# Routed experts: rows added to the output by accumulating scatters, in place of a stored table and a combining stage

## The reference

```
hn  = rmsnorm(h, g_ffn)
pg_top, g_idx = top_k(softmax(hn @ w_rg + b_rg), 1)           # 4 groups, the best one
pe_top, e_idx = top_k(softmax(le of that group), 2)           # its 8 experts, the best two
wts = pg_top * pe_top / sum(pe_top)
yb  = (silu(x @ w_gate[e]) * (x @ w_up[e])) @ w_down[e]       # blocks of 128 rows, one expert each
y   = h + sum over the row's two experts of wts * yb
```

## Time and profile before

| | us |
|---|---|
| median of 3 runs | 4226.6 (4226.56 to 4235.43) |
| the profiled execution | 4223.9 |
| its span | 4222.4 |
| expert blocks, from the first Silu to the last copy out of PSUM | 3133.8 to 4105.9 |
| `combine`, from its first load to the end of the span | 4111.9 to 4222.4 |

### The profile page before, as it was taken

One profiled execution on the slowest core, in us unless ns is written; L12 is line 12 of the kernel. 1 busy time (PEld: TensorE's weight loads), 2 busy tenths in 40 slices (PEclk: granted clock), 3 DMA queues, 4 the chain that ended last, 5 costly groups with the idle time before them and its releaser, 6 DMA issues. The chain is left out here.

```text
span 4222.4 us, 58476 instructions
## 1 busy us (share of the span) xinstructions
PE 3404.8 (81%) x20680; PEld 2601.9 (62%) x20729; DVE 2026.5 (48%) x2607; ACT 1367.8 (32%) x2483; POOL 741.7 (18%) x552
## 2 busy tenths in 40 slices
PE   7988759999978888835868996688758999989980
PEld 5777647777756666522426774377647777777760
DVE  3666635555544333331116662233266766675634
ACT  4555433333325323311212322244213433333320
POOL 1333200000000000022100001011114444453423
PEclk9999879999989888966878997788769999999995
DMA  6667543333333111225423332232257967786748
GB/s 223 234 230 236 202 157 138 131 133 138 135 105 96 56 41 51 66 66 168 147 82 112 126 118 91 79 96 97 87 180 248 335 242 254 270 299 217 284 188 319
DMA packets 302568, 683.64 MB, mean 162 GB/s; under 512 B 83355, under 2 KB 95051, under 8 KB 296238
## 3 DMA queue, kind: packets, MB, share of 16 engines
q1 hardware_dynamic: 229910, 448.38, 31.0%
q0 software_dynamic: 53936, 192.71, 13.4%
q10 hardware_dynamic: 18576, 40.51, 2.5%
HBM read 522.60 MB, written 193.16 MB: 170 GB/s over the span
## 5 line engine op out<-in xcount | busy, mean ns | idle before, releaser
L136 PE MATMUL inu_po<-inu_w,inu_nT 128*128 128x512 f32 (+1 forms) x680 | 253.8, 373 | 57.6 <-DVE inu_nT L131 42.1
L2674 POOL TENSOR_TENSOR ex_down<-ex_down_raw,ex_down 128x2048 fp32r<-128x2048 f32 x32 | 205.5, 6422 | 455.7 <-ACT ex_down L2750 455.7
L137 PE MATMUL inu_po<-inu_w,inu_nT 128*128 128x512 f32 (+1 forms) x680 | 247.6, 364 | 0.0
L138 PE MATMUL inu_po<-inu_w,inu_nT 128*128 128x512 f32 (+1 forms) x680 | 247.5, 364 | 0.0
L535 DVE TENSOR_REDUCE att_res<-att_score 128x4 f32<-128x1024 f32 (+1 forms) x96 | 92.5, 988 | 272.3 <-DMA tmp_att<-att_res 221.7
L607 PE MATMUL att_outp<-att_va,att_pT 128*128 128x65 f32 x1200 | 184.5, 300 | 46.9 <-DVE att_pT L542 46.4
L2777 ACT ACTIVATE ex_late<-ex_py 128x512 f32<-128x512 f32 x96 | 52.3, 597 | 485.0 <-PE ex_py L138 485.0
L607 PEld LDWEIGHTS att_outp<-att_va,att_pT 128*128 128x128 f32 x1200 | 170.1, 216 | 63.6 <-DVE att_pT L542 57.8
L136 PE MATMUL inq_po<-inq_w,inq_nT 128*128 128x512 f32 x408 | 192.9, 473 | 19.0 <-DVE inq_w L1082 19.0
L136 PE MATMUL ex_py<-ex_down,ex_hT 128*128 128x512 f32 x384 | 155.9, 406 | 57.0 <-POOL ex_down L2674 44.4
L248 POOL DMA_DIRECT2D inu_big<-tmp_u x256 | 137.5, 538 | 298.9 <-DVE inu_big L324 252.9
(11 more groups left out here) (570 smaller groups left out, 8414.6 us busy)
## 6 DMA issues: line engine op xcount, KB each, us to landing
ex_gate_raw<-in_w_gate SPq DMA_DIRECT2D x32, 2048.0 KB
ex_up_raw<-in_w_up SPq DMA_DIRECT2D x32, 2048.0 KB, 12.0
ex_down_raw<-in_w_down POOLq DMA_DIRECT2D x32, 2048.0 KB, 9.3
inu_big<-tmp_u POOLq DMA_DIRECT2D x256, 192.0 KB, 3.5
tmp_yb<-ex_late ACTq DMA_DIRECT2D x48, 512.0 KB, 7.6
tmp_nT<-inu_nT SPq DMA_DIRECT2D x17, 1024.0 KB, 4.9
inq_nT<-tmp_nT SPq DMA_DIRECT2D x17, 1024.0 KB, 5.0
out_win_k<-in_cache_k SPq DMA_DIRECT2D x8, 2032.0 KB
```

The lines of the kernel that those rows point to most:

```text
L136: pe.matmul(out, ah, bh, start=start, stop=False)
L137: pe.matmul(out, ah, bl, start=False, stop=False)
L138: return pe.matmul(out, al, bh, start=False, stop=stop)
L2674: return eng.tensor_tensor(half["d"][:, 1, k], raw["d"][:, k], half["d"][:, 0, k].bitcast(F32), ALU.subtract)
```

## The change

The stage `combine` and the scratch tensors `yb`, `i_dst`, `wts` and `h2` go. `attend_memory` writes the residual rows straight to the output `y`. The scratch rows `hn` become 1024 + 32 numbers wide: behind each row lie its 32 expert weights, 30 of them zero (`dense`), and a row of zeros stands in front of all rows, for padding. `dense` is made by DVE (three operations of 128x544, and four small ones that stood later before), stored by SP. The gathers bring 4224 bytes a row instead of 4096. ACT copies the block's column of weights to `shares` and uses it as the scale of the copies out of PSUM. In place of the store to `yb`, POOL issues an indirect DMA that adds the block's 128 rows to `y` in memory. Padding rows are added to the rows behind the last real one, for which `y` has one more tile; their lane-wise row numbers are made by five small DVE operations. Since a row's two experts may lie in neighbouring blocks, each add waits for the one before it to have landed. The zero stores go.

```
@@ SP @@
-                sp.wait_ge(E["placed"], 1)
-                sp.dma_start(t["i_dst"], dsti[:]).then_inc(E["saved"], 16)
+                sp.wait_ge(E["zero_ok"], 1)
+                sp.dma_start(t["hn"][0:1, :], zero[0:1, 0:D + NE]).then_inc(E["dense_out"], 16)
+                sp.wait_ge(E["dense_ok"], 1)
+                sp.dma_start(t["hn"][1:, D:].rearrange("(n p) e -> p n e", p=P), dense).then_inc(E["dense_out"], 16)
...
-                def nothing(b):
-                    sp.dma_start(t["yb"][b], zero).then_inc(E["zero_out"], 16)
@@ POOL @@
+                pool.memset(zero, 0.0).then_inc(E["zero_ok"], 1)
+                pool.wait_ge(E["zero_ok"], 1)
+                for u, half_of in enumerate((slice(0, P // 2), slice(P // 2, P))):
+                    pool.dma_start(t["y"][NT, half_of], zero[half_of, 0:D]).then_inc(E[f"y_out{u}"], 16)
+                pool.wait_ge(E["dense_out"], 32)
                 pool.wait_ge(E["idx_ok"], 1)
                 for u in range(SLOTS):
-                    gather(u, idx[:, u:u + 1])
-                pool.memset(zero, 0.0).then_inc(E["zero_ok"], 1)
+                    gather(u, start[:, u:u + 1])
...
+                pool.wait_ge(E["rows_ok"], 1)
+
+                def add(i, u, b):
+                    pool.wait_ge(E["y_ok"], 2 * b + 4)
+                    pool.sem_inc(E["seen"], 1)
+                    pool.wait_ge(E[f"y_out{1 - u % 2}"], i * 32 + (u + 1) // 2 * 16 + 16)
+                    pool.sem_inc(E["seen"], 1)
+                    pool.indirect_dma_start(t["y"].rearrange("n p d -> (n p) d"), bass.IndirectOffsetOnAxis(ap=spot[:, u, 1:2].bitcast(U32), axis=0),
+                                            y[:, u % 2, :], None, compute_op=ALU.add).then_inc(E[f"y_out{u % 2}"], 16)
                 def work(i, u, b):
                     pool.wait_ge(E["x_turned"], b + 1)
-                    pool.tensor_copy(spot[:, u, :], idx[:, bass.ds(b + SLOTS, 1)]).then_inc(E["spot_ok"], 1)
+                    pool.tensor_copy(spot[:, u, :], rows_of[:, bass.ds(b, 1), :].rearrange("p n a -> p (n a)")).then_inc(E["spot_ok"], 1)
+                    pool.wait_ge(E["shares_ok"], b + 1)
...
+                    add(i, u, b)
@@ ACT @@
                     act.wait_ge(E["gate_mm"], b + 1)
+                    act.activation(shares[:, u % 2], xb[:, u, bass.ds(expert(act, b) + D, 1)], ACT.Copy).then_inc(E["shares_ok"], 1)
                     act.wait_ge(E["hh_ok"], b + 1)
                     act.activation(sg, gu[:, 0, :], ACT.Silu).then_inc(E["sg_ok"], 1)
...
                     for n in range(2):
-                        act.activation(y[:, u % 2, 512 * n:512 * n + 512], py[:, n, :], ACT.Copy).then_inc(E["y_ok"], 1)
-                    act.wait_ge(E["y_ok"], 2 * b + 4)
-                    act.dma_start(t["yb"][b], y[:, u % 2, :]).then_inc(E[f"y_out{u % 2}"], 16)
+                        act.activation(y[:, u % 2, 512 * n:512 * n + 512], py[:, n, :], ACT.Copy, scale=shares[:, u % 2]).then_inc(E["y_ok"], 1)
@@ DVE @@
+                for a in range(2):
+                    own.then(V((dense, dense1)[a], oh[:, a], bn(wts[:, a], NE), ALU.mult))
+                V(dense, dense, dense1, ALU.add).then_inc(E["dense_ok"], 1)
                 dve.wait_ge(E["sums_ok"], 1)
...
+                    if a:
+                        dve.wait_ge(E["y_out0"], 16)
+                        dve.wait_ge(E["y_out1"], 16)
+                        dve.wait_ge(E["dense_out"], 32)
...
                 rows(1, 1)
+                own.then(TS(pad[:, 1], pad[:, 0], 0.0, None, ALU.is_equal))
...
+                dve.tensor_copy(rows_of[:, :, 1], pad[:, 0]).then_inc(E["rows_ok"], 1)
                 lower("u", 1)
-def combine(nc, t):
...
```

More of the change, by code:

```diff
@@ L2646, in route_experts @@
         nb, starts, base, cmp = (few[:, k] for k in range(4))
+        dense, dense1 = (byt(spots1[:, D + NE + a * NT * NE:D + NE + (a + 1) * NT * NE]) for a in range(2))
         def read(eng, row, b, top):
@@ L2821, in _ @@
                 own.then(dve.tensor_reduce(m[:, 0], g4[:, 1], AXX, ALU.add))
+                own.then(TS(m[:, 7], m[:, 6], 1.0, None, ALU.add))
+                own.then(V(m[:, 0], m[:, 0], m[:, 7], ALU.mult))
+                own.then(dve.reciprocal(wts[:, 0], m[:, 0]))
+                own.then(V(wts[:, 1], wts[:, 0], m[:, 6], ALU.mult))
+                for a in range(2):
+                    own.then(V((dense, dense1)[a], oh[:, a], bn(wts[:, a], NE), ALU.mult))
+                V(dense, dense, dense1, ALU.add).then_inc(E["dense_ok"], 1)
                 dve.wait_ge(E["sums_ok"], 1)
@@ L2853, in _ @@
                     V(marks[:, a], marks[:, a], bn(tok, NBX), ALU.mult).then_inc(E["marks_ok"], 1)
+                    if a:
+                        dve.wait_ge(E["y_out0"], 16)
+                        dve.wait_ge(E["y_out1"], 16)
+                        dve.wait_ge(E["dense_out"], 32)
                     V(spots[a], row(ib, P), bn(posf[:, 0, a], P), ALU.is_equal).then_inc(E["spots_ok"], 1)
                 dve.wait_ge(E["idx_mm"], 1)
-                dve.tensor_copy(idx[:], th[:, 0:NBX]).then_inc(E["idx_ok"], 1)
-                here = tok[:, 0:1].to_broadcast([P, NE])
+                dve.tensor_copy(start[:], th[:, 0:SLOTS]).then_inc(E["idx_ok"], 1)
+                own.mark(dve.tensor_copy(rows_of[:, :, 0], th[:, SLOTS:SLOTS + NBLK]))
+                own.mark(dve.tensor_copy(pad[:, 0], th[:, 0:NBLK]))
+                own.mark(TS(lane[:, 1:2], tok[:, 0:1], float(SEQ + NS), None, ALU.add))
+                own.then(TS(lane[:, 0:1], tok[:, 0:1], -1.0, None, ALU.add))
+                here = lane[:, 0:1].to_broadcast([P, NE])
                 own.then(V(cmp, ends, here, ALU.is_le))
@@ L2863, in _ @@
                 dve.tensor_reduce(cols[:, 1:2], cmp, AXX, ALU.add).then_inc(E["cols_ok"], 1)
-                own.then(TS(m[:, 7], m[:, 6], 1.0, None, ALU.add))
-                own.then(V(m[:, 0], m[:, 0], m[:, 7], ALU.mult))
-                own.then(dve.reciprocal(wts[:, 0], m[:, 0]))
-                own.then(V(wts[:, 1], wts[:, 0], m[:, 6], ALU.mult))
                 dve.wait_ge(E["plan_mm"], 1)
@@ L2886, in _ @@
                 rows(1, 1)
+                own.then(TS(pad[:, 1], pad[:, 0], 0.0, None, ALU.is_equal))
+                own.then(TS(pad[:, 1], pad[:, 1], lane[:, 1:2], None, ALU.mult))
+                own.mark(TS(pad[:, 0], pad[:, 0], -1.0, None, ALU.add))
+                own.wait()
+                own.then(V(pad[:, 0], pad[:, 0], pad[:, 1], ALU.add))
+                dve.tensor_copy(rows_of[:, :, 1], pad[:, 0]).then_inc(E["rows_ok"], 1)
                 lower("u", 1)
@@ L3193 @@
     out = {n: r[f"out_{n}"] for n in OUTPUTS}
-    flat = {n: out[n].reshape((ROWS, -1)) for n in ("k", "v", "y")}
+    flat = {n: out[n].reshape((-1, out[n].shape[-1])) for n in ("k", "v", "y")}
     return (flat["y"][:SEQ].reshape(1, SEQ, D), flat["y"][SEQ:SEQ + NS].reshape(DEC_B, DEC_T, D),
```

103 lines of the change are left out of this document (22 added, 81 removed).

## The result

| | before | after |
|---|---|---|
| median, us | 4228.1 (4226.56 to 4235.43, 4 runs) | 4186.9 (4170.96 to 4205.53, 4 runs) |
| profiled execution / its span | 4223.9 / 4222.4 | 4198.9 / 4197.4 |
| start of the first copy out of PSUM | 3165.41 | 3172.30 |
| start of the last one | 4104.82 | 4186.92 |
| from there to the end of the span | 117.6 | 10.5 |

The ratio is 0.9894, with a 95% interval of 0.9865 to 0.9923: faster by about 1%, 41 us in the medians where 90 were forecast. The range (4104 to 4195) holds it, the likeliest case's own range (4113 to 4165) doesn't.

A forecast was written before the change was run, and what follows sets the result against it. PE was taken as near its own pace over 48 blocks, with 116.5 us behind the last: 4223.9 - 108.3 + 1 + 1 + 12 + 4 = 4133.6, with 2.7 added 4136 us; range 4104 to 4195.

The forecast's parts named there:

- the likeliest case: The forecast itself for the whole kernel: 4136 us, own range 4113 to 4165, chance 0.55.
- the tail: Behind the last block: 116.5 us replaced by 8.2, with 7 for the add's landing; -108.3 us (-100 to -111).
- the head: Start of the expert stage: small operations numbering padding rows delay the first up weights; +1.0 us (0 to +8).
- Rival C: Blocks: an add lands later than a block lasts, past 20.9 us; slower than before, 4409 at 25 us; chance 0.08.
- DMA traffic: Single-block experts: the add's extra read costs 1.4 us in a DMA-bound block; +4 us (0 to +11).
- POOL's lateness: Long series of single-block experts: DVE's work delays the add's issue and POOL's half; +12 us (0 to +24).
- ACT's chain: Copy out of PSUM to ACT's down weights: 17 first blocks at -0.4 us, 8 at +1.0; +1 in all.
- POOL's part: POOL's queue behind the add: in time by about 1.4 us, late only in long series; +12 us, elsewhere nothing.
- The stretch from the first Silu to the last copy: Sign over the expert blocks, 972 us before: growth above 45 us or shrinkage above 5 means wrong in the main.
- PE's wait on POOL: Sign at the down projection, on POOL's `lower_d`, 44.4 us before: 45 to 75 forecast, 30 or less a shorter chain.
- rival A: Chain to the down weights gets shorter, 23 second blocks of pairs gain 0.5 to 0.8 us; 4107 us, chance 0.13.
- Rival B: Add costly on the DMA engines, 5.7 us a block; 68 instead of 4 over 17 single-block experts; 4200, chance 0.23.

The follow-up runs named there:

- The forced order: The changed kernel with POOL's half of the down weights made to wait for DVE's half, so DVE's comes first: 4127.3 us, ratio 0.9761.
- the plain write: The changed kernel with DVE's half first and the scatter writing instead of adding: 4114.0 us, ratio 0.9729.
- the kernel with the order forced and early reads: The changed kernel with DVE's two plan reads ahead of its wait for Silu and up, and POOL's half waiting for DVE's: 4104.5 us, ratio 0.9704.

## Why the prediction was wrong

In the profiled execution the sum missed by 65.3 us (4198.9 against 4133.6). The turned blocks of both kernels make 62.8 of the stretch's growth, the other blocks 12.4, where 17 were forecast for the whole stretch; the earlier stages add 9.4 to the miss, the tail 1.2, and the head takes 3.5 off. (The ends of the prediction's terms add up to 4117 to 4171, not to its 4113 to 4165; the measured time lies outside both.)

**The tail, right.** 108.3 forecast, 107.1 measured. The add's landing was taken as 7 us; the last one, with nothing else under way, took 6.0, as the shortest of all (min, median, max):

```profile
DMA to landing us min/median/max: 6.0/10.0/14.3
```

Rival C needed more than 20.9; it is out.

**The head, right in its range**: +1 forecast, -2.5 measured. The row that answers to the earlier trace rows shows DVE's idle time for PE's sums fallen from 3.94 us to 0.67, so the new operations lay where they were put:

```profile
3090.31 0.09 DVE L2840 MEMSET ex_xb<- 128x32 f32 x1 [0.67 <-PE ex_gu L2945]
```

**DMA traffic and POOL's lateness, right in size.** +4 and +12 forecast. The 32 blocks that are turned in neither kernel grew by 12.4 together, and blocks 1, 16, 22 and 40 alone make that much (3.3, 3.3, 3.6 and 2.7); the rest cancel. In block 16 the add's issue takes 4.49 us beside DVE's gate weights, as forecast from the earlier trace rows (nine of the 48 adds have an issue of 4.4 to 5.2 us), and ACT's part, behind two table loads, ends at +9.32 and is last:

```profile
3495.91 4.49 POOL L2731 DMA_INDIRECT out_y<-ex_late,ex_spot  x1 [6.41 <-ACT ex_late L2791]
```

How much of it is POOL's, ACT's or the weights' was not separated.

**ACT's chain and the order of the two halves: the failed step.** There are two errors. The first is a size, in ACT's part. For a second block of a pair the prediction took -0.4 us from copy to down weights, "3895.24 - 3891.49 = 3.75" becoming 3.35. It became 3954.43 - 3952.32 = 2.11: Silu came 0.44 earlier as expected, but behind it ACT's 1.46 us of reading the plan shrank to 0.26, which the prediction left standing. Over the 23 blocks of this kind ACT's part ends 1.2 us earlier in the mean. The count of table loads, 48 of 1.28, was right, and so was their cost in the 8 blocks of the other kind: +1.0 forecast, +1.1 in the mean (from +0.6 to +2.0).

The second decides, and stands in POOL's part: "partly hidden, since DVE's own half of the down weights holds POOL up for 2 us anyway", and "elsewhere nothing". The prediction saw in the earlier trace rows a POOL half of 6.69 us that was held for 2.29, and took the order for a property of the kernel. It came about because both engines stood waiting for ACT, and DVE's wait ended 0.05 us before POOL's, in 28 of the 31 first blocks. The prediction worked out when POOL would be ready (some 5.6 us behind the copy; it was 7.2) and ACT's part (7.0; it was 5.7), but never when DVE would. With the true 5.7 for ACT, the order hangs on 7.2 against 7.7. The prediction looked for POOL's lateness in the long series, where POOL comes too late to be first; the loss fell on the experts with two blocks, where it is in time. So a term of +73 stands where the sum has nothing. The three blocks of before with POOL first, of 24.9 to 25.8 us, lay in its trace and gave the price: 5 to 6 us a block. The forced order gives 60 us back in the medians (4186.9 to 4127.3).

**The marks set.** The stretch from the first Silu to the last copy was to grow by no more than 45, and grew by 69 (1041.0). PE's wait on POOL was to be 45 to 75 or, if the chain was shorter, 30 or less; it was 38.4, and the time had moved to a wait on `hT` that no mark looked for. ACT's chain was in fact shorter, as rival A said, and that gave POOL room to be first. It wasn't needed everywhere: in block 5 ACT's part came at +6.98, as forecast, and POOL at +7.06, but DVE, which needed 1.32 us from its product to its half, only at +7.38. How much of the turning is ACT's and how much DVE's slower reads was not separated. Rival B is priced by the plain write at 13 us, with 21 at the upper end of the scatter, where it wanted 68. The stated range of 4104 to 4195 was as wide as it was for rival B's sake. That it holds the result is luck, since what filled it was a term that it didn't contain.

The changed kernel's runs spread over 35 us, those with the order forced over 14. A different number of turned blocks from run to run would explain it, but it is not shown: the kernel with the order forced and early reads spreads over 31, and the kernel before over 31 to 46 in its three sets.

## What to carry to other kernels

Where VectorE and GpSimd work on the same buffer behind one semaphore, work out the arrival of all three parties, not of the one whose queue is changed: an engine that comes earlier can turn the order of the other two. An order that rests on two waits for the same event is worth fixing with a wait or an earlier read, so that the engine is first behind which more is queued. A few odd blocks in the trace of the kernel before (three of 31 first blocks here) are the price list of what the change may make common.

## What the runs showed of the hardware

A 128x2048 subtraction takes 2.29 us on DVE and 4.59 on POOL when first, and the second of the two ends its own 2.2 us (DVE) or some 4.5 us (POOL) behind the first. An accumulating scatter of 128 rows of 4 KB costs POOL 1.61 us of issue and the plain one 1.00, as a gather; it lands in 10.0 us in the median beside the weights' loads and in 6.0 alone. Its issue rises to 2.6 to 5.2 us where DVE works on the gate weights. DVE's first read of a number of the plan in a block took 0.53 to 1.31 us in the twelve turned blocks, where it takes 0.30 to 0.32 in the others but one. In block 37 a wait of 5.07 us for PE was followed by about 4.4 us of matmuls at the lower clock, in the kernel before one of 1.52 us by none.
